# Reordering the pair preparation, the attention outputs and the block substitution of a hybrid RWKV-7 and sparse attention layer

## The reference

```python
# RWKV-7 branch, 8 heads of 64; decay, a, k, kk, r per token and head
kk = k * k_k;  kk = kk / max(|kk|, 1e-12);  k = k * (1 + (a - 1) * k_a)
def step(S, inp):
    sa = einsum('bhij,bhj->bhi', S, -kk_t)
    S = S * w_t + sa x (kk_t * a_t) + v_t x k_t
    return S, einsum('bhij,bhj->bhi', S, r_t)
y = group_norm(y) + sum(r * k * r_k) * v          # the last term: "bonus"

# sparse attention branch, 8 heads, keys c_kv (latent), 128 best keys of each query
score = where(causal, sum_h(w_i * relu(q_idx . k_idx)), -inf); _, idx = top_k(score, 128)
s = where(valid, q_abs . c_sel, -inf);  o = softmax(s) @ c_sel @ w_uv
y_attn = o * silu(gate)
```

## Time and profile before

| | us |
|---|---|
| median of 3 runs | 1468.22 |
| lowest and highest of them | 1466.9 and 1473.95 |
| the profiled execution, its own time | 1469.24 |
| its span | 1467.4 |
| PE busy in the span | 1408.8 |
| DVE busy in the span | 933.8 |

### The profile page before, as it was taken

One profiled execution on the slowest core, in us unless ns is written; L12 is line 12 of the kernel. 1 busy time (PEld: TensorE's weight loads), 2 busy tenths in 40 slices (PEclk: granted clock), 3 DMA queues, 4 the chain that ended last, 5 costly groups with the idle time before them and its releaser, 6 DMA issues.

```text
span 1467.4 us, 18610 instructions
## 1 busy us (share of the span) xinstructions
PE 1408.8 (96%) x7612; PEld 1144.1 (78%) x7612; DVE 933.8 (64%) x1322; ACT 487.7 (33%) x663; POOL 487.6 (33%) x131
## 2 busy tenths in 40 slices
PE   7999978699998999999999999999989999999997
PEld 6778646587888877888888887878878888888886
DVE  6679868735413357769969974762457888885122
ACT  5443367243324232122222223322233333332121
POOL 0004110012535323343434433334423443443441
PEclk9999999799999999999999999999989999999999
DMA  6221000023314211232232231222222223222221
GB/s 206 87 87 58 29 2 2 4 85 118 129 71 144 87 58 58 86 100 102 86 105 97 87 115 58 86 98 104 86 87 86 87 88 113 87 99 95 84 96 58
DMA packets 21349, 125.14 MB, mean 85 GB/s; under 512 B 2384, under 2 KB 3408, under 8 KB 7696
## 3 DMA queue, kind: packets, MB, share of 16 engines
q1 hardware_dynamic: 20752, 121.71, 23.6%
q10 hardware_dynamic: 512, 2.23, 0.4%
HBM read 121.84 MB, written 2.10 MB: 84 GB/s over the span
## 4 chain that ended last, share of the span: by engine, by line
PE 88%; DVE 8%; ACT 3%; issue 1%; DMA 0%; DVEq 0%; SPq 0%; ACTq 0%
PE bank L402 25%; PE bank L404 24%; PE bank L403 24%; PE bank L1008 1%; PE bank L1024 1%; PE bank L354 1%; DVE conv_b L2406 1%; PE bank L393 1%; ACT prob L1409 1%; PE bank L877 1%; PE bank L958 1%; PE bank L626 0%; ACT probT L1415 0%; PE bank L362 0%; DVE op_hi L1736 0%
## 5 line engine op out<-in xcount | busy, mean ns | idle before, releaser
L1204 POOL TENSOR_TENSOR w_lo<-w_raw,w_hi 128x2048 fp32r<-128x2048 f32 (+1 forms) x102 | 468.2, 4590 | 762.8 <-ACT w_hi L1256 746.9
L402 PE MATMUL bank<-op_hi,w_hi 128*128 128x512 f32 x1344 | 529.8, 394 | 6.4 <-DVE op_lo L1758 2.3
L404 PE MATMUL bank<-op_hi,w_lo 128*128 128x512 f32 x1344 | 525.9, 391 | 0.0
L403 PE MATMUL bank<-op_lo,w_hi 128*128 128x512 f32 x1344 | 525.9, 391 | 0.0
L402 PEld LDWEIGHTS bank<-op_hi,w_hi 128*128 128x128 f32 x1344 | 253.6, 189 | 63.7 <-issue 6.3
L404 PEld LDWEIGHTS bank<-op_hi,w_lo 128*128 128x128 f32 x1344 | 253.3, 188 | 54.6
L403 PEld LDWEIGHTS bank<-op_lo,w_hi 128*128 128x128 f32 x1344 | 253.4, 189 | 54.0 <-issue 0.7
L1256 ACT ACTIVATE w_hi<-w_raw 128x2048 fp32r<-128x2048 f32 (+2 forms) x109 | 205.6, 1887 | 265.3 <-PE bank L404 265.3
L2299 DVE SCALAR_TENSOR_TENSOR bank<-pad_b,par,bank 128x512 f32<-128x512 f32 x232 | 175.3, 756 | 7.8
L2465 DVE TENSOR_TENSOR tmp<-tmp,conv_f 128x512 f32<-128x512 f32 x22 | 101.6, 4617 | 16.4 <-ACT tmp L1682 16.4
L2196 DVE TENSOR_TENSOR x_res<-bank,x_res 128x512 f32<-128x512 f32 x24 | 16.5, 691 | 136.9 <-PE bank L404 136.8
(11 more groups left out here) (374 smaller groups left out, 1702.0 us busy)
## 6 DMA issues: line engine op xcount, KB each, us to landing
w_raw<-in_w_units SPq DMA_DIRECT2D x104, 1024.0 KB, 4.9
w_raw<-in_w_units SPq DMA_DIRECT2D x4, 768.0 KB, 4.2
x_res<-in_x SPq DMA_DIRECT2D x8, 256.0 KB, 6.5
x_res<-in_x ACTq DMA_DIRECT2D x2, 1024.0 KB, 6.3
out<-x_res SPq DMA_DIRECT2D x8, 256.0 KB, 2.2
w_raw<-in_w_units SPq DMA_DIRECT2D x3, 512.0 KB, 9.0
w_raw<-in_w_units SPq DMA_DIRECT2D x4, 256.0 KB, 5.6
mem_tok<-in_mem SPq DMA_DIRECT2D x1, 1024.0 KB, 5.2
```

Of the source, the lines that this page charges most:

```text
L402: nc.tensor.matmul(b[:, 0:width], h, xh[:, x0 + k, 0:width], start=start and k == ks[0], stop=False)
L403: nc.tensor.matmul(b[:, 0:width], h, xl(x0 + k, width), start=False, stop=False)
L404: mm = nc.tensor.matmul(b[:, 0:width], l, xh[:, x0 + k, 0:width], start=False, stop=stop and k == ks[-1])
L1204: nc.gpsimd.tensor_tensor(w_lo[u % 2][:, 0:nk, :], w_raw[u % 2][:, 0:nk, :], w_hi[u % 2][:, 0:nk, :].bitcast(F32), ALU.subtract).then_inc( ...
```

## The change

It changes no computation. It has five parts:

1. `decay_and_rate` and what follows use `prep[0]` and `prep[1]` for even pairs and two new tiles `prep_odd` for odd ones (`decay_home`). On ACT the wait for the pair ahead moves from `decay_and_rate` to `decays`, and to pair i - 2 in the former. ACT's `decays(1)` stands ahead of `strict_upper(0)`, `decays(2)` and `decays(3)` further ahead as well.
2. On PE `strict_upper` stands ahead of `scores` of the same pair, and both of pairs 2 and 3 ahead of the attention outputs of pairs 0 and 1. `head_inputs(3)` and `scores(3)` come last.
3. On DVE all four pairs are prepared first. `heads_out` of pairs 0 and 1, `maxima(3)` and `probs(2)` now stand inside the substitution, behind its first 9 steps. `heads_out(3)` stands behind `blocks_out`.
4. The grams of chunks 0 and 1 are taken out of PSUM by ACT without a mask, and POOL masks them in place (`affine_select`); DVE's eight L2058 of these chunks go. PE waits for `gram_masked`.
5. On PE `heads_out(3)` stands ahead of `token_major(1)` and `value_grams(1)`.

```diff
+        prep_odd = [at(f"prep_odd{j}", 102400 + 2048 * j, [T]) for j in range(2)]
...
+        def decay_home(i, j):
+            return prep_odd[j][:, 0:T] if i % 2 else prep[j][:, 0:T]
...
             def value_products(c, i2):
...
-                for odd in range(2):
-                    evacuated(pe, ("gk", c, odd, i2))
+                if c < 2:
+                    pe.wait_ge(sem("gram_masked"), 4 * c + 2 * i2 + 2)
+                else:
+                    for odd in range(2):
+                        evacuated(pe, ("gk", c, odd, i2))
...
+            strict_upper(0)
             scores(0)
-            strict_upper(0)
...
             probabilities_turned(NI - 1)
+            heads_out(NI - 1)
             token_major(1)
             value_grams(1)
-            heads_out(NI - 1)
             chunk_values(1)
...
+            def grams_masked(c):
+                for i2 in range(2):
+                    for odd in range(2):
+                        h = NI * odd + 2 * i2
+                        evacuated(pool, ("gk", c, odd, i2))
+                        g = g_k[:, h:h + 2, :, :]
+                        nc.gpsimd.affine_select(out=g, in_=g, compare_op=ALU.is_ge, fill=0.0, base=-1,
+                                                pattern=[[0, 2], [1, 2], [1, P]], channel_multiplier=-1).then_inc(sem("gram_masked"), 1)
...
             def decay_and_rate(i):
+                if i >= 2:
+                    act.wait_ge(sem("prep_ready"), i - 1)
+                    act.wait_ge(sem("bk_decayed"), 2 * i - 2)
+                elif i == 1:
+                    filled(act, ("ga", 1, 1))
...
+            def decays(i):
+                act.wait_ge(sem("cum_ready"), i + 1)
                 if i:
                     act.wait_ge(sem("prep_ready"), i)
                     act.wait_ge(sem("bk_decayed"), 2 * i)
...
+            def value_grams(c):
+                for i2 in range(2):
+                    if c:
+                        filled(act, ("yv", c - 1, i2))
+                    for odd in range(2):
+                        h = NI * odd + 2 * i2
+                        b = take(act, ("gk", c, odd, i2))[:, :].rearrange("p (n a t) -> p n a t", n=2, a=2)
+                        evac(A(g_k[:, h:h + 2, :, :], b, ACT.Copy), ("gk", c, odd, i2))
...
+            key_terms(3)
+            decayed(3)
+            maxima(2)
+            probs(1)
             blocks_in()
-            substitution(0, 8)
-            probs(NI - 1)
-            value_grams(0, 0)
-            value_grams(0, 1)
+            substitution(0, 9)
+            heads_out(0)
+            heads_out(1)
+            maxima(3)
+            probs(2)
+            substitution(9, 16)
             heads_out(NI - 2)
-            substitution(8, 16)
-            value_grams(1, 0)
-            value_grams(1, 1)
+            probs(3)
+            substitution(16, 24)
+            substitution(24, BLK - 1)
+            blocks_out()
             heads_out(NI - 1)
-            substitution(16, BLK - 1)
-            blocks_out()
```

More of the change, by code:

```diff
@@ L767, in _ @@
             norms_spread(1)
+            strict_upper(0)
             scores(0)
-            strict_upper(0)
+            key_bonus(1)
+            decay_and_rate(2)
+            norms_spread(2)
             head_values()
[L771 to L782, removed]
+            head_inputs(1)
+            key_bonus(2)
+            strict_upper(1)
+            scores(1)
+            decay_and_rate(3)
+            norms_spread(3)
+            probabilities_turned(0)
+            key_bonus(3)
+            strict_upper(2)
+            head_inputs(2)
+            strict_upper(3)
+            scores(2)
+            heads_out(0)
+            probabilities_turned(1)
+            heads_out(1)
+            head_inputs(3)
+            scores(3)
             def chunk_values(c, before_second=None):
@@ L1426, in _ @@
             decay_and_rate(1)
+            decays(1)
             strict_upper(0)
-            decays(1)
+            decay_and_rate(2)
+            exps(0)
+            decays(2)
             head_values()
[L1430 to L1439, removed]
+            head_inputs(1)
+            strict_upper(1)
+            decay_and_rate(3)
+            exps(1)
+            decays(3)
+            turned(0)
+            strict_upper(2)
+            head_inputs(2)
+            strict_upper(3)
+            turned(1)
+            exps(2)
+            head_inputs(3)
+            def value_grams(c):
[6 more added lines that the diff above has]
+                        evac(A(g_k[:, h:h + 2, :, :], b, ACT.Copy), ("gk", c, odd, i2))
             def value_products(c, i2):
@@ L1968, in key_terms, with bonus_value @@
                     .then_inc(sem("rk_ready"), 1)
-                V.scalar_tensor_tensor(prep[1][:, 0:T], prep[1][:, 0:T], 1.0, prep[0][:, 0:T], ALU.add, ALU.mult).then_inc(sem("b_ready"), 1)
+                V.scalar_tensor_tensor(decay_home(i, 1), decay_home(i, 1), 1.0, decay_home(i, 0), ALU.add, ALU.mult).then_inc(sem("b_ready"), 1)
+            def bonus_value(i):
+                b = take(dve, ("bonus", i))
+                evac(V.tensor_tensor(bonus_v[:, i, :], b[:, :], vf[:, i, :], ALU.mult), ("bonus", i))
             def decayed(i):
@@ L1974, in decayed @@
                                 ALU.mult)
-                V.scalar_tensor_tensor(chunked(ar[:, i, 0, :]), chunked(prep[0][:, 0:T]), -2.0, e_down[:, :, 0:P], ALU.mult, ALU.mult)
-                b = take(dve, ("bonus", i))
-                evac(V.tensor_tensor(bonus_v[:, i, :], b[:, :], vf[:, i, :], ALU.mult), ("bonus", i))
+                V.scalar_tensor_tensor(chunked(ar[:, i, 0, :]), chunked(decay_home(i, 0)), -2.0, e_down[:, :, 0:P], ALU.mult, ALU.mult)
+                if i != 2:
+                    bonus_value(i)
                 dve.wait_ge(sem("rk_ready"), i + 1)
@@ L2080, in _ @@
             decayed(1)
[L2081 to L2090, removed]
-            blocks_in()
-            substitution(0, 8)
-            probs(NI - 1)
-            value_grams(0, 0)
-            value_grams(0, 1)
+            key_terms(2)
+            bonus_value(2)
+            maxima(1)
+            decayed(2)
+            probs(0)
+            key_terms(3)
+            decayed(3)
+            maxima(2)
+            probs(1)
+            blocks_in()
+            substitution(0, 9)
+            heads_out(0)
+            heads_out(1)
+            maxima(3)
+            probs(2)
+            substitution(9, 16)
             heads_out(NI - 2)
-            substitution(8, 16)
-            value_grams(1, 0)
-            value_grams(1, 1)
+            probs(3)
+            substitution(16, 24)
+            substitution(24, BLK - 1)
+            blocks_out()
             heads_out(NI - 1)
-            substitution(16, BLK - 1)
-            blocks_out()
             for half in range(2):
```

22 lines of the change are left out of this document (13 added, 9 removed).

## The result

The changed kernel is slower: a median of 1477.6 us against 1469.7 us for the kernel before, 20 runs each, a ratio of 1.0046 with a 95% interval of 1.003 to 1.0061. By the ratio that is +6.8 us (the two medians themselves differ by 7.9). The forecast was 1463, and the measured time lies outside its range of 1455 to 1471. Its times spread from 1468.45 to 1483.02; those of the kernel before from 1466.9 to 1476.66. The profiled execution took 1475.24, with a span of 1473.4.

The account below looks back on a forecast made before the run. It took DVE's list up to `blocks_out` to bound the stage, then PE's list ahead of L729. -5.5 (waits), +1.9 and -1.8 (clock) sum to -5.4, from 1469.24 profiled, 1.0 above the median, to 1463; range 1455 to 1471.

Parts of the forecast that it names:

- The list of waits: Changed instruction lists of four engines, followed with their waits: side products start at 272.9 against 278.40, -5.5 us.
- PE's idle time of about 7 us: From 222 to 229, PE's last two transposes of pair 1 wait for banks holding pair 0's output until DVE frees them.
- DVE's wait for `heads_out(1)`: Inside the substitution, behind step 9: transposes, ACT's copy, L626, L633 and signals come to 5.2 us, to 234.5.
- The wait that replaced the removed one: PE's list ahead of L729: grams of chunk 1 need the bank freed by DVE's heads_out(3), which ends at 266.7.
- Term (a): PE's new idle time from 222 to 229 may lower the clock for work from 229 to 239: half of 3.8, +1.9.
- Term (b): The low clock behind 278 goes if PE is not idle long ahead of L729: half of at most 3.7, -1.8.
- stays down into the corner blocks: Named as making the forecast wrong: the clock falls behind a new idle time and stays low; no size or chance given.
- The start of the substitution: blocks_in from 239.6 to 219.9: waits -9.7 (7.0 of 16.7 us idle kept), stretch -3.7, moved work -6.3.
- The mask: POOL's mask of 512 columns: 1.18 us, four times a 128-column row's 0.29; lower end 0.44, upper some 3.5.
- The second rival: POOL's four masks of chunk 0 stretch DVE's steps 17 on, by 2.4 us (up to 4.0): 1467, chance 0.20.
- The third rival: The mask is dear and the kernel slower, from 1.9 us per mask; at 3.0 us 1472.5; chance 0.10.

Follow-up runs that it names:

- after_again: The changed kernel run once more, unedited, as control: median 1480.6 us, ratio 1.0042 against the kernel before.
- out3_first_filled: out3_ahead plus 15 and 14 repeated transposes in PE's idle time at pair 0 alone: median 1466.6 us, ratio 0.9957 against the kernel before.
- front_filled: The changed kernel plus 94 repeated transposes in PE's idle times at pairs 0 and 1 and ahead of the first masked grams: 1467.9 us, ratio 0.9962.
- mended order: out3_ahead with DVE's heads_out(0) ahead of the substitution, maxima(3) and probs(2) behind step 13, no repeats: 1460.3 us, ratio 0.9922 against the kernel before.
- out3_ahead: The changed kernel with DVE's heads_out(3) ahead of blocks_out instead of behind it: median 1468.7 us, ratio 0.9983 against the kernel before.

## Why the prediction was wrong

**The list of waits was right in its order.** PE's idle time of about 7 us lay where it was put, behind the bank that was named. At full clock DVE's wait for `heads_out(1)` was 5.43 (forecast 5.2). The wait that replaced the removed one was the one that was named too: from the end of `heads_out(3)` at 276.05 to L729 are 4.9 us, forecast 6.2.

**The step that failed is the clock, in both its terms.** Term (a), +1.9, looked at one new idle time and took half of 3.8. It missed the idle times ahead of 211, 2.29 and 2.01 us long with 0.6 us of work between them. At the low clock the work behind them took 2.7 us longer (L578 to L591: 2.08 + 2.08 + 0.89 + 2.65 against 1.12 + 1.16 + 0.76 + 1.99), and `blocks_in` came 2.7 us later by it. The second idle time cost 2.4 us in DVE's wait (7.84 against 5.43). Together that is 5.1 us in place of 1.9.

**Term (b) had the wrong sign.** It expected the low stretch behind 278 to go or halve, for -1.8. In the profiled execution it did go: from L729 to the first corner block (L756) are 12.9 us, against 17.1 before. That gain of 4.2 is more than the 3.7 that the prediction called the most, since it had left out L722 itself (3.62 at the low clock, 2.21 at the full one). But another low stretch began at 292 and lasted until 305, with PE busy all the time, where before one had ended at 296. From the first corner block to the scan are 24.9 us against 19.8, which is +5.1 and turns a lead of 1.6 us into a lag of 3.5. The remaining 2.5 of the 6.0 between the two spans came behind 1080, where the program is the same in both kernels (PEclk 0.68 against 0.74 from 1080 to 1100, and 0.78 in after_again), so that part goes with the execution and not with the order. The prediction had named this case, the clock that "stays down into the corner blocks", as what would make it wrong, and had given it no price and no chance.

**The trace of the kernel before had the warning.** Three of its idle times are near 2 us:

```profile
187.11 0.88 PE L653 MATMUL bank<-ar,bt 64*32 64x32 f32 x64 [2.06 <-DVE soft L2013]
...
249.58 1.08 PE L684 MATMUL bank<-tok_v,g_k 128*128 128x64 f32 x8 [2.10 <-DVE g_k L2058]
...
291.30 0.21 PE L734 MATMUL bank<-inv_dia,z 32*32 32x32 f32 x1 [1.92 <-issue]
```

Behind the first PEclk is 0.70 and 0.50 (186 to 190), behind the last 0.66 and 0.50 (292 to 296), and behind the middle one it stays at 1.00, as it does behind one of 2.61 us ahead of 198.80. The prediction set 7 us against 12.61 and left idle times of this size without a price.

**The start of the substitution was mis-sized too, apart from the clock.** Of DVE's 16.7 us idle the forecast kept 7.0. In the changed kernel the same waits came to 12.1, and to 9.6 with the first idle time filled (out3_first_filled: 1.14, 2.72, 0.49 and 5.27). So of the 5.2 us by which `blocks_in` was late (225.1 against 219.9) some 2.6 are waits that were there at full clock as well (of the 9.6 us 8.0 are for scores), and 2.7 are the clock. From 272.9 to the 281.0 of the side products the parts are: 5.2 for `blocks_in`, 2.6 for the wait for `heads_out(1)` (7.84 against 5.2), 0.9 for steps 17 to 31, 0.6 in small pieces, and 1.3 less behind `heads_out(3)`, most of it the cheaper mask.

**The steps that were off without deciding.** The mask was priced at 1.18 from one row and took 0.64 at the median. The Trainium skill's rule (GPSIMD Engine Reference, section 4.1, Engine selection: one input at roughly line rate), by which the estimate had been 0.6, was the better guide. The second rival, the stretch of the substitution, was real but small: three instructions of steps 17 and 18, which run while POOL masks, took 0.68 to 0.74 where 0.42 stands behind them, 0.9 us in all for four masks against a bound of 4.0. Steps 17 to 31 took 12.1 in place of 11.2 in the changed kernel and in front_filled alike. The third rival, a mask above 1.9 us, did not occur. The kernel was slower by another mechanism.

**What stays open.** Why a low stretch lasts 5 us in one place and 13 in another while PE is busy, why 1.38 us idle is followed by a long one and 2.10 by none, and why the same idle time of 2.07 us is followed by one in some executions and not in others, no run here settles. The landmarks of each kernel come from one execution, so single starts are uncertain by what the clock did in it. Nor was it tried how much part 4 is worth in the mended order.

## What to carry to other kernels

Of a reordering, ask for every idle time of TensorE that it makes, not only for those on the chain of waits, and price behind each the work at the lower clock; an idle time of 2 us, once of 1.4, with little work around it was enough here. The trace of the kernel before can show this already. The first suspects are the banks: a reader that is moved back in its own list holds a bank, and the fix was to move readers (`heads_out(0)` and `heads_out(3)` further ahead, `maxima(3)` and `probs(2)` further back) rather than to take out work. To tell a clock from an order, fill the idle time with repeated products and compare the times of several runs, since the starts in a single profile also carry low stretches that have nothing to do with the edit. If the kernel gets faster, it was the clock.

## What the runs showed of the hardware

- More work on TensorE made the kernel faster: 95 repeated transposes took the kernel before down by 0.34%, 94 took the changed one down by some 12.7 us, and 94 took out3_ahead down by 10.2 us.
- The granted clock fell behind idle times of 2.0 to 2.3 us as well as behind those of 4 to 13 us, and also behind 1.92 us (before, ahead of 291.30) and 1.38 us (changed kernel, ahead of 290.13); behind 2.10 and 2.61 us (before, ahead of 249.58 and 198.80) it stayed at 1.00. A stretch at 1.2 GHz lasted from 3.5 us (out3_ahead, around 290) to some 17 (after_again, 275 to 292), with TensorE busy in most of it.
- The granted clock is not the same in two executions of one kernel. In ten runs each of one set the times spread over 14.4 us with the idle times (after_again) and over 5.5 with most of them filled (front_filled).
- A GpSimd mask (`affine_select`, 128 x 512, in place) takes 0.64 us at the median of eight (0.82 at most), and 0.29 for 128 columns.
